# VectorE in place of TensorE and ScalarE for the scaled residual of an inverse

## What is computed

```
lmat = jnp.where(strict, beta[..., :, None] * kk * decay, 0.0) + eye
t_inv = lax.linalg.triangular_solve(lmat, eye, left_side=True, lower=True, unit_diagonal=True)
u = jnp.einsum("bhnij,bhnjd->bhnid", t_inv, v * beta[..., None])
w = jnp.einsum("bhnij,bhnjd->bhnid", t_inv, k * (beta * jnp.exp(g))[..., None])
```

## Time and profile before

| what | value |
|---|---|
| median of 3 runs | 2354.21 us (2350.39 to 2355.19) |
| the profiled execution's own time | 2352.94 us |
| its span | 2351.1 us |
| PE busy | 2268.6 us, 96% |
| PEld busy | 1828.8 us, 78% |
| DVE busy | 1126.1 us, 48% |
| ACT busy | 841.9 us, 36% |
| POOL busy | 1145.8 us, 49% |

### The profile page before, as it was taken

How to read it: one execution, slowest core, us unless ns; L and a number is a source line. 1 busy time by engine, 2 the same in 40 slices (tenths; PEclk the granted TensorE clock), 3 DMA queues, 4 the chain that set the end, 5 groups by cost and what they waited for, 6 DMA issues and landing times.

```text
span 2351.1 us, 34310 instructions
## 1 busy us (share of the span) xinstructions
PE 2268.6 (96%) x13528; PEld 1828.8 (78%) x13528; DVE 1126.1 (48%) x1960; ACT 841.9 (36%) x2252; POOL 1145.8 (49%) x674
## 2 busy tenths in 40 slices
PE   8999999989999999999999999999899998999997
PEld 6787888877777788888777778778677787888885
DVE  4677677764444611110257776777544476111003
ACT  3554445465541211110145554454665403111100
POOL 5453333324337466666545432333343385666664
PEclk9999999999999999999999999999999999999999
DMA  4221112111123232332232211211111332323322
GB/s 151 72 81 46 50 55 60 42 50 46 55 89 135 72 97 91 99 99 90 92 108 72 72 46 42 64 50 42 50 47 53 109 116 90 98 91 98 117 90 81
DMA packets 53887, 182.65 MB, mean 78 GB/s; under 512 B 7520, under 2 KB 8160, under 8 KB 53728
## 3 DMA queue, kind: packets, MB, share of 16 engines
q1 hardware_dynamic: 48976, 167.01, 22.1%
q10 hardware_dynamic: 4752, 13.45, 1.6%
HBM read 169.94 MB, written 4.19 MB: 74 GB/s over the span
## 4 chain that ended last, share of the span: by engine, by line
PE 88%; DVE 8%; issue 2%; ACT 1%; DMA 1%; POOL 0%; DVEq 0%; ACTq 0%; POOLq 0%
PE PS L583 19%; PE PS L585 18%; PE PS L584 18%; PE PS L751 12%; PE PS L843 2%; PE PS L957 2%; PE PS L1024 2%; PE PS L829 2%; PE PS L847 2%; PE PS L971 1%; PE PS L902 1%; PE PS L886 1%; PE PS L780 1%; PE PS L893 1%; PE PS L923 1%
## 5 line engine op out<-in xcount | busy, mean ns | idle before, releaser
L544 POOL TENSOR_SCALAR wh<-w_raw 128x1024 fp32r<-128x1024 f32 (+1 forms) x255 | 278.1, 1091 | 1034.3 <-DMA w_raw<-stream 1033.4
L547 POOL TENSOR_TENSOR wl<-w_raw,wh 128x1024 fp32r<-128x1024 f32 (+1 forms) x255 | 615.0, 2412 | 21.3
L583 PE MATMUL PS<-xh,wh 128*128 128x512 f32 x992 | 398.8, 402 | 8.6 <-issue 4.2
L585 PE MATMUL PS<-xl,wh 128*128 128x512 f32 x992 | 390.2, 393 | 0.0
L584 PE MATMUL PS<-xh,wl 128*128 128x512 f32 x992 | 389.6, 393 | 0.0
L583 PEld LDWEIGHTS PS<-xh,wh 128*128 128x128 f32 x992 | 188.1, 190 | 56.0 <-issue 10.8
L585 PEld LDWEIGHTS PS<-xl,wh 128*128 128x128 f32 x992 | 188.1, 190 | 40.8
L584 PEld LDWEIGHTS PS<-xh,wl 128*128 128x128 f32 x992 | 188.5, 190 | 37.1
L751 PE MATMUL PS<-xh,wh 128*128 128x512 f32 x448 | 206.2, 460 | 5.2 <-DVEq L1690 3.4
L1993 DVE TENSOR_TENSOR hf<-sg,PS 128x512 f32<-128x512 f32 x44 | 30.2, 687 | 359.9 <-PE PS L585 359.9
L1643 DVE SCALAR_TENSOR_TENSOR conv_acc<-PS,cw,conv_acc 128x510 f32<-128x510 f32 x192 | 143.9, 749 | 99.3 <-ACT conv_acc L1186 93.9
(11 more groups left out here) (287 smaller groups left out, 4828.0 us busy)
## 6 DMA issues: line engine op xcount, KB each, us to landing
w_raw<-stream SPq DMA_DIRECT2D x254, 512.0 KB, 3.4
w_raw_spare<-stream SPq DMA_DIRECT2D x46, 512.0 KB, 3.4
x<-x_in ACTq DMA_DIRECT2D x6, 512.0 KB, 7.8
qx<-qx SPq DMA_DIRECT2D x48, 64.0 KB, 2.0
raw<-raw SPq DMA_DIRECT2D x32, 64.0 KB, 2.0
ln_g<-ln_rows ACTq DMA_DIRECT2D x4, 512.0 KB, 4.2
ln_b<-ln_rows ACTq DMA_DIRECT2D x4, 512.0 KB, 5.2
x_park<-x ACTq DMA_DIRECT2D x4, 512.0 KB, 4.1
```

What stands on the lines that cost most here:

```text
L544: nc.gpsimd.tensor_scalar(wh[s][:, w], w_raw[s][:, w], 1.0, 1.0, ALU.mult, ALU.mult).then_inc(w_hi_done, 1)
L547: nc.gpsimd.tensor_tensor(wl[s][:, w], w_raw[s][:, w], wh[s][:, w].bitcast(F32), ALU.subtract).then_inc(split_done, 1)
L583: mm(o, ah, bh, start=first, stop=False)
L585: return mm(o, ah, bl, start=False, stop=last)
```

## The change

The identity product goes from TensorE and the copy from ScalarE. The constant tile `id_16` becomes `id_e`, the identity times `E_SCALE` (1024). VectorE forms V in one instruction a direction, `sum * E_SCALE + id_e`, after `front_scale` and ahead of `fill_out` and `scaled_keys`.

```diff
-        id_16 = place("id_16", [P, P], F16)
+        id_e = place("id_e", [P, P], F16)
...
                     for r in range(2):
                         pe.wait_ge(y_upd[r], n * 7 + 7)
-                        mm(PS[:, 3 * r, :].rearrange("p (c t) -> p c t", c=CHUNKS), id_16[:], rows(id_16[:]), start=True,
-                           stop=False, skip_group_check=True)
                         for c in range(CHUNKS):
                             o = PS[:, 3 * r, c * P:(c + 1) * P]
-                            mm(o, NAh[r][:, c, :], Y[r][:, c, :], start=False, stop=False, skip_group_check=True)
-                            ins = mm(o, NAl[r][:, c, :], Y[r][:, c, :], start=False, stop=True,
-                                     skip_group_check=True)
+                            mm(o, NAh[r][:, c, :], Y[r][:, c, :], start=True, stop=False)
+                            ins = mm(o, NAl[r][:, c, :], Y[r][:, c, :], start=False, stop=True)
                         ins.then_inc(e_mm[r], 1)
...
-                    for r in range(2):
-                        act.wait_ge(e_mm[r], n + 1)
-                        A(V[r][:].rearrange("p c t -> p (c t)"), PS[:, 3 * r, :], ACT.Copy,
-                          scale=E_SCALE).then_inc(e_ready[r], 1)
...
-            nc.vector.tensor_copy(id_16[:], ident).then_inc(ready_bf, 1)
+            TS(id_e[:], ident, E_SCALE, None, ALU.mult).then_inc(ready_bf, 1)
...
                     if more:
                         front_scale(h + 1, n + 1, 1 - s)
+                    for r in range(2):
+                        dve.wait_ge(e_mm[r], n + 1)
+                        STT(V[r][:], bank(3 * r), E_SCALE, rows(id_e[:]), ALU.mult, ALU.add).then_inc(e_ready[r], 1)
                     fill_out(ISSUED[h, "L6"])
                     scaled_keys(n, s)
```

## The result

The change makes the kernel slower: 2369.73 us median (2366.14 to 2372.55, 4 runs) against 2353.16 (2350.39 to 2355.19), a ratio of 1.0072 with an interval of 1.006 to 1.0084. That is 16.6 us where 8.9 were forecast: the sign is right, the forecast is about half of what was measured, and the time lies above the range. The same kernel timed again later gave 2367.14 and 1.0057 (1.0044 to 1.007), 15.0 us more than the kernel before beside it. Of those six executions three took 2363.5 to 2364.6 us at a mean granted clock of 0.987 to 0.989, and three 2369.7 to 2370.0 at 0.985 or 0.986; both traces of the changed kernel are of the longer kind, so part of what they show of the clock may not be paid each time. The profiled execution has a span of 2369.1 us, 18.0 more than before.

What follows compares the result with a forecast made beforehand. The kernel was taken to be bound by how densely TensorE is fed. Terms -1.2 + 7.3 + 2.4 + 0.3 + 0.9 - 0.8 = +8.9 us gave 2361.8 from the profiled 2352.94, 2363.1 from the median; forecast 2362, range 2352 to 2368.

Steps and rivals of the forecast that it cites:

- What goes: On TensorE, 32 identity products of 0.21 us are saved: 6.7 us in all, 0.42 per head.
- ScalarE's copies cost nothing: Dropping ScalarE's pair of copies, 1.26 us in each of 16 heads, was costed at nothing, since TensorE works behind them.
- What comes: Two new VectorE instructions per head, 0.61 us a step, 1.22 for the pair, not held up by GpSimd.
- Heads like the third, and the last: Four heads undisturbed by GpSimd gain 0.29 us each (-1.2); the layers' last heads gain the whole 0.42 (-0.8).
- First and fifth heads: GpSimd's L547 gets ahead of VectorE's kb, so L902 starts later: +1.83 us in each of 4 heads, +7.3.
- the second rival: VectorE's pair delays, but L547 and L522 do not get ahead of kb and kn: -1.0 us, 2353; chance 0.12.
- What excludes is an instruction of VectorE with both inputs in SBUF: Claim that such VectorE instructions and GpSimd's L544 exclude each other; scaled kn takes 1.22 us in place of 0.56.
- Sixth heads: In the sixth head and its twin, kb is due just as GpSimd is done: 0.15 us each, +0.3.
- The step that failed: TensorE's loss up to the product with YF counted in full, the rest of each head unchanged; sum +8.9 us.
- fourth rival: A head's later part meets the lock elsewhere: two more blocks 3.7 us on top, 2366; four 2370; chance 0.10.
- The first rival: TensorE alone decides, YF is nowhere too late, and all 6.7 us come back: 2347.5; chance 0.08.
- The third, that lost time comes off later waits: TensorE's lost time comes off its later waits in a head, where VectorE catches up: at half, +4; chance 0.10.

## Why the prediction was right and wrong

- *What goes.* 0.21 us a product: right, 0.41 to 0.45 a head in 12 heads when the products alone are taken away. That the sum over 16 heads is then 6.7 as well is luck: the second heads gain nothing, and one sixth head gains 1.57.
- *ScalarE's copies cost nothing.* Right: the list of waits of the kernel before has none of TensorE for ScalarE's V, so nothing came back; VectorE's V is waited for by 0.6 us in sum.
- *What comes.* The pair at 0.61 a step and never held up: right, 1.27 for a pair, 0.673 to 0.692 us each in 32 instances, running beside L544 and L547.
- *Heads like the third, and the last.* Forecast -0.29 and -0.42; measured -0.32 and -0.41.
- *First and fifth heads.* +1.83 forecast. The first heads gave 1.81 and 1.83, the fifth 1.68 and 1.67. There kb went first and kn was caught, the case that the second rival names, with nearly the same loss, as it says.

```profile
375.07 0.54 DVE L1618 TENSOR_TENSOR kb<-kn,bdl 128x384 f32<-128x384 f32 x1
375.72 2.56 DVE L1618 TENSOR_TENSOR kn<-kn,bdl 128x384 f32<-128x384 f32 x1
...
374.94 2.92 POOL L547 TENSOR_TENSOR wl<-w_raw,wh 128x1024 fp32r<-128x1024 f32 x1
```

  kb starts 0.13 after L547 in these rows and still goes ahead. The rule of the Trainium skill that the prediction cites ("SBUF — State Buffer", "Who interferes with whom") holds for the exclusion; that whoever starts first has the port does not hold here by the starts that a profile shows. It changes the loss by 0.15 us a head. The prediction's "What excludes is an instruction of VectorE with both inputs in SBUF" is too narrow: the copy of ht has one input, and in the second head it takes 1.67 us beside a running L547 and 0.17 in the third. The prediction itself uses that wait, so its sum does not suffer.
- *Sixth heads.* +0.15 forecast, -0.09 and -0.47 measured. They were at the mercy of when GpSimd's work lands, by a few tenths.
- **The step that failed** is "What TensorE loses here I count in full, since the rest of a head is paced by TensorE". It set everything behind the product with YF to nothing. The runs put 7.8 us in its place in the heads. 3.2 is the lowered clock behind the fifth heads' waits, gone when those waits are taken away. 3.65 is the collision at the end of the first layer's fourth head with its own drop of the clock; it comes with the absence of the identity products and is gone when that unit is held back. What moves the landing of that unit stays open. The rest is small change of both signs. Outside the heads the trace has another 5.0 us between the layers, with 3.4 us more of the clock not granted, and 2.5 less elsewhere; no run isolates these.
- The prediction had this as its fourth rival, "meets the same lock elsewhere", with a chance of 0.10 and a price of 3.7 for two more blocks, and 2370 for four. One such collision did come, but through the landing of a unit of weights and not through a shifted head, and the clock, some 5 of the 7.8 us, stands in no case. That its 2370 is close to the measured time is luck. The range ended at 2368 for that reason.
- The first rival (all 6.7 back) is refuted by the 13.0 us of waits, the second by kb's 2.67. The third, that lost time comes off later waits, did not happen: the wait for V at L843 rose from 10.6 to 12.8.

## What to carry to other kernels

An engine's idle time right ahead of the one result that the busiest engine waits for is not room. Ask what stands between the new work and that result, and whether any of it can be shut out by another engine: here the split of six units of weights, moved by a few us, decided between 1.0057 and 0.9985. And a wait of TensorE of about 2 us is to be priced with a drop of its clock behind it, some 1.7 us more in this kernel, though not each time.

## What the runs showed of the hardware that was not expected

- The clock's answer to a wait has no simple length here. 1.96 us in the fifth head was followed by a drop, 2.08 in the first was not, 1.85 at the fourth head's end was in the changed kernel and was not without the identity products. Each drop took 1.6 to 1.7 us. What decides it these runs do not settle.
- The port passes to a waiting GpSimd behind an instruction of VectorE that reads two SBUF tiles, also when VectorE goes on at once with a read of PSUM. Putting two such reads between kn and kb was what opened the door: L544 began 0.29 after kn and ran 1.29 us in place of the 1.77 of the earlier trace rows, so L547 was ready ahead of kb.
